# Summing gathered expert rows as four 64x64 squares on TensorE, with longer lags and more rows in late attention

## The reference

```python
def block(args):                       # 128 tokens at a time
    xt, et, gt = args
    act = gelu(einsum('td,thkd->thk', xt, u[et]))
    return einsum('thk,thkd->td', gt * act, v[et])
```

## Time and profile before

| | |
|---|---|
| time, median of 3 runs | 3728.08 us |
| span of the profiled execution (first to last instruction) | 3488.4 us |
| median less that span | 239.7 us |
| TensorE busy | 2948.9 us (85%) |
| VectorE busy | 2349.6 us (67%) |
| ScalarE busy | 812.5 us (23%) |
| GpSimd busy | 2015.7 us (58%) |
| moved by DMA | 1345.09 MB |

### The profile page before, as it was taken

One profiled execution on the slowest core, in us unless ns is written; L12 is line 12 of the kernel. 1 busy time (PEld: TensorE's weight loads), 2 busy tenths in 40 slices (PEclk: granted clock), 3 DMA queues, 4 the chain that ended last, 5 costly groups with the idle time before them and its releaser, 6 DMA issues.

```text
span 3488.4 us, 34790 instructions
## 1 busy us (share of the span) xinstructions
PE 2948.9 (85%) x10984; PEld 1651.9 (47%) x10984; DVE 2349.6 (67%) x5893; ACT 812.5 (23%) x1915; POOL 2015.7 (58%) x2085
## 2 busy tenths in 40 slices
PE   7876898888988898889997899888998889976675
PEld 6465455544545355534554456444564445522222
DVE  6229846886588765886578765886648865596555
ACT  3111411132211421133211322114221232211111
POOL 1004755666566765666565655665556655477775
PEclk9898999999999999999999999998999999999998
DMA  7788999999999999999999999999999999999998
GB/s 279 277 274 313 408 409 409 408 409 409 409 407 406 394 409 409 408 407 382 409 409 408 392 356 409 409 409 348 359 409 409 409 355 342 385 404 410 409 409 347
DMA packets 386971, 1345.09 MB, mean 386 GB/s; under 512 B 41762, under 2 KB 44834, under 8 KB 386148
## 3 DMA queue, kind: packets, MB, share of 16 engines
q0 software_dynamic: 294912, 1073.87, 78.1%
q1 hardware_dynamic: 90724, 264.79, 20.0%
q10 hardware_dynamic: 1152, 4.19, 0.3%
HBM read 1332.99 MB, written 35.39 MB: 392 GB/s over the span
## 4 chain that ended last, share of the span: by engine, by line
PE 38%; DMA 30%; DVE 15%; POOL 9%; issue 6%; ACT 3%; SPq 1%; DVEq 0%; POOLq 0%; ACTq 0%
PE ps_sum L1267 18%; DMA rows<-in_peer_u,ids_u 13%; DMA rows<-in_peer_v,ids_v 10%; PE ps_p L999 5%; POOL rows L824 5%; POOL rows L810 4%; DVE rows L2052 4%; PE ps_s L1181 4%; DMA rows<-in_peer_v,ids_u 3%; DMA w_ring<-packed 3%; PE ps_s L1118 2%; PE ps_p L1126 2%; DVE feat_b L1935 1%; DVE feat_b L1931 1%; PE ps_s L1114 1%
## 5 line engine op out<-in xcount | busy, mean ns | idle before, releaser
L1267 PE MATMUL ps_sum<-rows,diag 128*128 128x512 f32 x3548 | 1727.6, 629 | 267.1 <-DMA rows<-in_peer_v,ids_v 141.4
L2052 DVE CUSTOM_DVE_ANT_0 rows<-h_cur,rows 128x1024 f32<-128x1024 f32 x1024 | 1226.8, 1220 | 496.3 <-DMA rows<-in_peer_u,ids_u 483.3
L810 POOL DMA_INDIRECT rows<-in_peer_u,ids_u x1024 | 1012.3, 989 | 702.0 <-issue 483.3
L1267 PEld LDWEIGHTS ps_sum<-rows,diag 128*128 128x128 f32 x3548 | 671.0, 200 | 1155.7 <-issue 1005.7
L824 POOL DMA_INDIRECT rows<-in_peer_v,ids_v x512 | 490.3, 958 | 433.8 <-PE ps_sum L1267 277.6
L824 POOL DMA_INDIRECT rows<-in_peer_v,ids_u x512 | 498.2, 973 | 284.7 <-PE ps_sum L1267 144.2
L1528 ACT ACTIVATE diag<-ident,acts 128x128 f32<-128x128 f32 x887 | 324.7, 394 | 1049.4 <-PE ps_sum L1267 750.1
L999 PE MATMUL ps_p<-hT,w_ring 128*128 128x128 f32 x2944 | 358.7, 282 | 28.8 <-DMA w_ring<-packed 15.3
L999 PEld LDWEIGHTS ps_p<-hT,w_ring 128*128 128x128 f32 x2944 | 353.0, 198 | 61.2 <-issue 39.7
L1834 DVE CUSTOM_DVE_ANT_0 e<-ps_s,bias_t 128x256 f32<-128x256 f32 (+6 forms) x96 | 74.2, 773 | 176.3 <-PE ps_s L1118 73.7
L2074 DVE SCALAR_TENSOR_TENSOR x_cur<-rows,acts,x_cur 128x1024 f32<-128x1024 f32 x137 | 175.6, 1282 | 7.4 <-DMA rows<-in_peer_v,ids_v 7.3
(11 more groups left out here) (288 smaller groups left out, 2376.2 us busy)
## 6 DMA issues: line engine op xcount, KB each, us to landing
w_ring<-packed SPq DMA_DIRECT2D x343, 512.0 KB
w_ring<-in_wstream SPq DMA_DIRECT2D x65, 512.0 KB
packed<-in_wstream SPq DMA_DIRECT2D x49, 512.0 KB, 8.2
rows<-in_peer_u,ids_u POOLq DMA_INDIRECT x1024, 14.9
rows<-in_peer_v,ids_u POOLq DMA_INDIRECT x512, 12.6
rows<-in_peer_v,ids_v POOLq DMA_INDIRECT x512, 19.3
bias_rows<-rows SPq DMA_DIRECT2D x5, 1024.0 KB, 12.1
bias_t<-in_x SPq DMA_DIRECT2D x8, 512.0 KB, 7.9
```

The source lines that it names most:

```text
L810: pool.indirect_dma_start(u_rows[:, slot, :], None, peer_u, bass.IndirectOffsetOnAxis(ap=ids_u[:, j:j + 1], axis=0)).then_inc(u_landed[slo ...
L1267: ins = pe.matmul(ps_sum[:, c * 512:(c + 1) * 512], diag[:, n % 4, :], v_rows[:, slot, c * 512:(c + 1) * 512], start=(j == 0), stop=(n == ...
L2052: dve.tensor_tensor_reduce(row, h_cur[:, :], row, 1.0, 0.0, ALU.mult, ALU.add, dots[:, p:p + 1]).then_inc(u_used, 1)
```

## The change

V rows are no longer multiplied by a full diagonal matrix but by its two 64x64 diagonal squares, kept side by side as `diag` of 64 columns. Four matmuls of a 64x64 square by 512 columns take the place of two of 128x128: square (c, r) reads rows r of the partitions and column half c of the row, and writes to partition half c of bank r. `sum_out` puts the four quarters back with four additions. VectorE adds rows only in the last block; elsewhere all go to TensorE. The ring of diagonals has 7 places. The four lags grow by 2, 4, 5 and 5. The stops from position 27 to 89 are shifted by `later`: by up to `MORE_ROWS` at position 53, falling to none at 27 and 89. The base tables keep the numbers of before.

```diff
 def on_vector(b, j):
-    return j % SHARE == SHARE - 1 or (b == NB - 1 and j >= TAIL and j % 2)
+    return b == NB - 1 and (j % SHARE == SHARE - 1 or (j >= TAIL and j % 2 == 1))
...
+ATTEND, JOINED, RANKED = 27, 53, 89
+def later(table, more):
+    def moved(p):
+        up, down = (p - ATTEND) / (JOINED - ATTEND), (RANKED - p) / (RANKED - JOINED)
+        return p + math.floor(more * max(0.0, min(up, down)) + 0.5)
+    return {name: tuple(moved(p) for p in stops) for name, stops in table.items()}
+MORE_ROWS = (0, 0, 1, 3, 6, 9, 9)
+TENSOR_STOPS, VECTOR_STOPS, SCALAR_STOPS = ([later(at, more) for more in MORE_ROWS] for at in (TENSOR_AT, VECTOR_AT, SCALAR_AT))
...
-GATE_LAG = 1
-DIAG_LAG = STEP + 2
-SUM_LAG = STEP + 5
-GATHER_LAG = STEP + 4
+GATE_LAG = 3
+DIAG_LAG = STEP + 6
+SUM_LAG = STEP + 10
+GATHER_LAG = STEP + 9
+DIAGS = 7
...
-        diag = sb("diag", [P, 4, P])
+        diag = sb("diag", [P, DIAGS, P // 2])
+        ident_halves = sb("ident_halves", [P, P // 2])
...
-                    for c in range(2):
-                        ins = pe.matmul(ps_sum[:, c * 512:(c + 1) * 512], diag[:, n % 4, :], v_rows[:, slot, c * 512:(c + 1) * 512],
+                    for c, r in ((0, 0), (0, 1), (1, 0), (1, 1)):
+                        own = slice(64 * r, 64 * r + 64)
+                        ins = pe.matmul(ps_sum[64 * c:64 * c + 64, r * HALF:(r + 1) * HALF], diag[own, n % DIAGS, :],
+                                        v_rows[own, slot, c * HALF:(c + 1) * HALF],
...
-                    act.wait_ge(v_used, n + SUM_SLOTS - 3)
-                    act.activation(diag[:, n % 4, :], ident[:, :], ACT.Copy, scale=coef[:, j:j + 1]).then_inc(diag_made, 1)
+                    ge(act, v_used, n + SUM_SLOTS + 1 - DIAGS)
+                    act.activation(diag[:, n % DIAGS, :], ident_halves[:, :], ACT.Copy, scale=coef[:, j:j + 1]).then_inc(diag_made, 1)
...
             def first_norm():
+                act.wait_ge(consts_made, 3)
+                for r in range(2):
+                    own = slice(64 * r, 64 * r + 64)
+                    copy(ident_halves[own, :], ident[own, own]).then_inc(halves_made, 1)
+                act.wait_ge(halves_made, 2)
                 square_x(0, 0)
...
-                dve.tensor_tensor(x_cur[:, :], x_cur[:, :], ps_sum[:, :], ALU.add).then_inc(fin_sum, 1)
+                for c, r in ((0, 0), (1, 1), (0, 1), (1, 0)):
+                    own = x_cur[64 * r:64 * r + 64, c * HALF:(c + 1) * HALF]
+                    ins = dve.tensor_tensor(own, ps_sum[64 * c:64 * c + 64, r * HALF:(r + 1) * HALF], own, ALU.add)
+                ins.then_inc(fin_sum, 1)
```

More of the change, by code:

```diff
@@ new lines @@
+TENSOR_AT = {
+    "latents": (1,), "mla_up": (9,), "gates": (17, 18), "recur": (20, 26), "mla_0": (29, 30, 31), "mla_1": (31, 31, 32),
+    "mla_2": (32, 33, 35), "mla_3": (35, 35, 37), "diff_0": (37, 38, 40, 41), "diff_1": (41, 43, 43, 44),
+    "diff_2": (45, 47, 48, 49), "diff_3": (49, 49, 51, 51), "join": (54, 56), "mix_out": (56, 56, 58, 58, 58),
+    "norm_cross": (59, 62), "cross_q": (62, 62, 62, 67, 67), "cross_scores": (69,), "cross_mix": (70, 73, 74),
+    "cross_out": (75, 75, 76, 78, 81), "norm_ffn": (83, 83), "peer_q": (83, 83, 85, 86, 88), "peer_scores": (89,),
+    "next_norm": (93, 99), "next_0": (104, 104, 106, 106), "next_1": (106, 106, 108, 108, 108),
+    "next_2": (112, 121, 121, 121, 121), "next_3": (121, 121, 124, 126, 126), "next_4": (126, 128, 128),
+}
@@ new lines @@
+VECTOR_AT = {
+    "latents": (0, 6), "mla_up": (8,), "conv": (17,), "gates": (19, 19, 21, 23), "recur": (25, 26), "mla_0": (26,),
+    "mla_1": (29,), "mla_2": (33,), "mla_3": (39,), "diff_0": (39, 39, 39), "diff_1": (42, 42, 43), "diff_2": (43, 45, 48),
+    "diff_3": (50, 52, 52), "join": (53, 54), "mix_out": (54, 55, 57, 57), "norm_cross": (59, 59, 63), "cross_scores": (71,),
+    "cross_mix": (71, 72), "cross_out": (73, 76, 84, 84), "norm_ffn": (85, 85, 85), "next_square": (90, 93),
[3 rows of a table added]
+}
+SCALAR_AT = {
+    "latents": (1, 7), "mla_up": (10,), "gates": (14, 18, 20), "mla_0": (28, 30), "mla_1": (30, 30), "mla_2": (32, 32),
+    "mla_3": (32, 34), "diff_0": (34, 38, 42), "diff_1": (42, 42, 42), "diff_2": (47, 47, 48), "diff_3": (48, 51, 53),
+    "norm_cross": (59,), "cross_q": (59, 60, 67), "cross_scores": (71,), "cross_mix": (73, 73, 74), "norm_ffn": (82,),
+    "peer_q": (82, 84, 88), "next_square": (90,), "peer_scores": (90,), "next_0": (104, 109), "next_1": (114, 114),
+    "next_2": (117, 120), "next_4": (125, 125), "choose_1": (125, 125),
+}
@@ L413, in program @@
         ones_made = sem("ones_made")
+        halves_made = sem("halves_made")
         ahead_made = sem("ahead_made")
```

99 lines of the change are left out of this document (removed), and 39 rows, old and new, of tables (SCALAR_STOPS, VECTOR_AT, VECTOR_STOPS).

## The result

The changed kernel takes **3832.23 us** (median of 4 runs, 3808.64 to 3836.14), the kernel before 3734.85 (4 runs, 3722.39 to 3741.9): 1.0285 of before, 95% interval 1.0242 to 1.0327. The forecast was 3675. The profiled execution took 3831.7 us, of which 3829.7 are its span.

A forecast was written before the change was run, and what follows sets the result against it. DMA at 409 GB/s was taken to bound all but the late attention and middle stretches, which are TensorE's. Span 3488.4 - 55 + 1.5 = 3435, plus 239.7 outside it: 3675 us (3674.8), 8-in-10 range 3648 to 3740.

The forecast's parts named there:

- the base of the sum: Whole run: profiled span 3488.4 us as starting point, plus 239.7 us by which the median exceeds the span.
- Rows off VectorE: 112 rows go from VectorE to TensorE, freeing 143 us of VectorE; worth nothing outside late 6, since DMA covers it.
- The squares: Row sums on TensorE: four squares overlap, 0.90 us a row instead of 1.72, plus switches between tile shapes; chance 0.71.
- Clock: Rival, late attention and middle: less busy TensorE gets a lower clock, 57 us lost, 3731 in all; chance 0.05.
- Diagonals: ScalarE's diagonals: half the columns and 7 places instead of 4 can only cost it less; priced at nothing.
- Lags: Sums, gathers and block-end work come later, coefficient, diagonal and sum each by 2 to 3 rows; all priced at nothing.
- More rows: Late attention: up to nine rows moved from the middle, 23.0 us of DMA; with faster rows, gain 55 of 79 us.
- `sum_out`: Block sums: one addition of 1.22 us becomes four, 2.7 us; seven covered by DMA, the last costs 1.5 us.
- the start: Before the first square: two small ScalarE copies and a GpSimd wait, about half a microsecond, covered by ScalarE's wait for x.
- Held back in order: Rival, `add_row`: program order makes squares wait for each other, 1.72 us a row plus switches, 4,000 us; chance 0.14.
- the signs named: Right if: eight records in about 0.9 us, attention 4 to 6 at 400 GB/s or more, GpSimd's attention waits nearly gone.
- The sign of being wrong: Middle 0 below 405 GB/s, or the squares' records still 0.43 us apart.

The follow-up runs named there:

- e1: The kernel before, unchanged, profiled again: 3707.58 us against 3705.4 for the same kernel, ratio 1.0002.
- e7: The change, but VectorE keeps every eighth row as before: 3736.79 us, 1.0099 of before.
- e5: The change as it is, run again on another occasion: 3780.57 us, 1.0219 of before.
- e12: Before with the squares, longer lags and ring of 7 half diagonals; no moved rows, every eighth row on VectorE: 3772.75 us, 1.0123 of before.
- e8: The change with MORE_ROWS all 0, so no row moved into late attention: 3805.33 us, 1.0274 of before.
- e9: Before with every fourth row of a block but the first on VectorE instead of every eighth: 3758.2 us, 1.0083 of before.
- e10: The change with every fourth row of a block but the first on VectorE: 3798.55 us, 1.0181 of before.
- e6: Before with each row summed by two 128x64 matmuls, half the array time, same instruction count on TensorE: 3725.63 us, 1.0057 of before.
- e14: Before with two 128x64 matmuls a row, plus a zero-adding filler matmul behind rows outside attention and middle: 3740.58 us, 1.0072 of before.
- e17: Before with two 128x64 matmuls for rows outside attention, the two long 128x128 ones kept inside it: 3742.47 us, 1.0047 of before.
- e2: Before with only the four 64x64 squares, half diagonals and quarter additions; ring of 4, lags and VectorE's rows as before: 3741.51 us, 1.0093 of before.
- e3: The change with two 128x64 matmuls a row (8 instructions) instead of four squares (16): 3752.38 us, 1.0120 of before.
- e18: Before with the four squares and a ring of 7 half diagonals instead of 4, lags as before: 3777.0 us, 1.0172 of before.

## Why the prediction was wrong

**The step that failed first is the base of the sum**: "Span 3488.4 - 55 + 1.5 = 3435; with the 239.7 us by which the median exceeds the span". It put 240 us outside the span, where no engine's wait could touch them. In e1 they are inside it: a usual execution has a span of 3714.7, with some 245 us more of GpSimd's stops. All that the prediction held to be covered by DMA was read from an execution in which no completion was late. In the usual one (e1) the rate is 405 GB/s at the most in any of the 28 stretches of the loop, and what was priced at nothing has a price. What the execution of the earlier trace rows itself took, and why it was so different, stays open.

**Rows off VectorE**, "Outside late 6 this is worth nothing, since DMA covers it": the largest part, 44 us from e7 to e5 and again 1.5%, give or take 0.7, from e12 to e8. GpSimd's waits for V slots grow by about as much, by 43 us (718 to 761) and by 61 (735 to 796). In the table both pairs of executions lose ahead of attention, 588 to 616 us and 585 to 616; alone each would be within what executions differ by. Why a row costs GpSimd more when TensorE sums it wasn't tried further: e9 and e10 show only that giving VectorE more than one in eight doesn't win it back.

**The squares**, 0.90 us a row: right as a price at 2.4 GHz (0.86 from row to row), wrong in what it is worth. e6 has the short row without the additional instructions: some -47 by the prediction's sums, +20 measured. The rival *Clock* had the loss but not the way to it. It had attention entered at a lower clock, but e14 enters attention 6 at 0.85 and e17 at 0.71, and the clock there goes by the rows inside: 0.75 with short ones, 0.95 with long ones. The argument against it ("in those stretches TensorE stays 85% busy or more") failed: attention 6 was 89% busy in e6 and still at 0.71. That its price, 57 us, would about use up the gain is luck: it was spread over attention and middle, and in e6 against e1 attention is 15 us longer but the middle 20 shorter. That the squares double the instructions costs another 0.36%, give or take 0.47 (e2 against e6), or 1.0, give or take 0.85 (e5 against e3): likely, but not resolved.

**Diagonals**, "Priced at nothing": the ring of 7 costs 0.8%, give or take 0.5 (e18 against e2). **Lags**, "All at nothing": some 10 us more at the end; over the whole run not to be told from a small gain. **More rows** gain 0.2 to 0.55%, inside the intervals (e12 to e7, e8 to e5); with the short rows they were to win 55 us. `sum_out` and the start weren't tried alone; the change's trace has the four additions at 0.69 us each, as priced, and the two copies at the start inside ScalarE's wait for x.

The steps from before to the change by e6, e2, e18, e12, e7, e5: +0.57, +0.36, +0.79, -0.49, -0.24, +1.20, in all 2.19% (e5; 2.85 where the change was first timed). The first, the third and the last are clear of their intervals; none of them is a gain of the forecast's size.

**Held back in order**, the rival on the other side, didn't happen; the time came out slower by other ways. Of the signs named, eight records in about 0.9 us came; 400 GB/s in attention 4 to 6 did not (305, 297 and 317), nor did GpSimd's waits vanish: it waits 813 us for V slots where e1 has 666, VectorE's rows included. The sign of being wrong came too: middle 0 is at 374 GB/s.

**Open**: what makes completions late. Bunches are absent from the one execution of the earlier trace rows and present in all 19 others. Where they are, records of semaphore updates are missing too, and idle instructions cost on all three engines tried. That would fit a path that they share, but no run singles one out. Loading the code is too small by its bytes: the page's busier instruction queue moves 2.03 MB in the change and 1.46 in e1, 1.4 us at 409 GB/s; whether an engine waits for such a load no view shows. The Trainium skill ("NOTIFIC — the notification-queue block", "Overflow: three behaviours, one of which stalls the engine") says that the block that writes the records of events holds up its producers when it is full inside. No run here can show that this is the cause. Nor is it known why the ring of 7 costs; no version here beat the kernel before.

## What to carry to other kernels

Set the profiled execution's span against the timed runs before building on it; where they differ by 6%, profile again, for the stretches that look saturated may be so in that execution alone. Work that is taken off TensorE can lower its granted clock for all that is left there (0.95 to 0.71 in attention 6, e1 to e6): price the rest of the stretch at both levels before counting the gain. And "hidden by DMA" has to be read from a usual execution, stretch by stretch.

## What was not expected of the hardware

- Four increments of a semaphore by TensorE came within 0.18 us, the last 4.5 us after the modelled end of its row (e1).
- TensorE's instructions of every kind, semaphore ones too, come at steps of 0.70 us or small multiples for 3 to 20 us at a time under the gathers: some 69 stretches, 482 us in the change, none in the profile of the earlier trace rows.
- Some 6,100 semaphore instructions on SyncE cost 43 us, though TensorE waits no longer for weight tiles; 7,100 on ScalarE cost 83, 7,100 on TensorE 76.
- TensorE's granted clock can fall to 0.71 in a stretch in which it is 89% busy (e6, attention 6; 0.95 with long rows, at 88%).
- Four 64x64 squares run at once: 8 records in 1.09 us, and a row every 0.86 us at 2.4 GHz.
